# Stationary values in the sparse attention, identity products in TensorE's waits, earlier loads, and eight modulation tiles moved

## What is computed

```python
# first block: three branches over the same queries, and one over other queries
o_cmp, p_cmp = compressed_branch(qn, kc_cmp, vc_cmp)      # 31 compressed keys
o_sel = selected_branch(qn, ks_r, vs, sel_idx)
o_win = window_branch(qn, kw_r, vw)
o_nsa = g0 * o_cmp + g1 * o_sel + g2 * o_win
o_dsa = dsa_branch(qd, kd, v_d, qi_r, ki_r, wi)           # the 128 highest of the scored keys
x = x + concat(o_nsa * silu(z_n), o_dsa * silu(z_d)) @ w_out
# second block, layer i of 2; m = the 9 modulation vectors of layer i (mc: of the context)
m = split(silu(c) @ w_ada[i] + b_ada[i], 9)
h = h + 0.5 * m[2] * swiglu(modulate(rms_norm(h), m[0], m[1]), w13, w2)
z = modulate(rms_norm(h), m[3], m[4]) @ w_in[i]
h = h + m[5] * (concat(fourier, latent attention, spatial gating, pooling) @ w_out[i])
h = h + 0.5 * m[8] * swiglu(modulate(rms_norm(h), m[6], m[7]), w13, w2)
```

## Time and profile before

| | |
|---|---|
| median of 3 runs | 3424.47 us |
| the profiled execution | 3433.63 us, of which the profile's span is 3431.9 us |
| TensorE busy | 3162.7 us of the span (92%) |
| VectorE busy | 1799.3 us (52%) |
| ScalarE busy | 839.1 us (24%) |
| GpSimd busy | 127.0 us (4%) |
| mean granted TensorE clock | 0.928 of full |
| HBM | 82 GB/s over the span |

### The profile page before, as it was taken

One profiled execution on the slowest core, in us unless ns is written; L12 is line 12 of the kernel. 1 busy time (PEld: TensorE's weight loads), 2 busy tenths in 40 slices (PEclk: granted clock), 3 DMA queues, 4 the chain that ended last, 5 costly groups with the idle time before them and its releaser, 6 DMA issues. The chain is left out here.

```text
span 3431.9 us, 41816 instructions
## 1 busy us (share of the span) xinstructions
PE 3162.7 (92%) x17560; PEld 2715.4 (79%) x17560; DVE 1799.3 (52%) x2690; ACT 839.1 (24%) x1019; POOL 127.0 (4%) x96
## 2 busy tenths in 40 slices
PE   7847988999999978989999999999999888899998
PEld 6745877788888866667888888788888675589996
DVE  4656565475554654555444433764645555553434
ACT  3322223421111222313211212321211223132222
POOL 2320122000000000000000000000000000000000
PEclk9975557999999999989999999999999998899999
DMA  4342001343332312022323222343433210233231
GB/s 138 88 119 95 13 13 56 104 129 123 108 119 86 110 39 70 1 67 80 104 92 92 92 68 61 96 135 97 126 98 95 83 50 17 73 92 96 88 90 58
DMA packets 340316, 288.27 MB, mean 84 GB/s; under 512 B 12896, under 2 KB 315488, under 8 KB 339168
## 3 DMA queue, kind: packets, MB, share of 16 engines
q1 hardware_dynamic: 340192, 286.58, 28.2%
HBM read 279.72 MB, written 2.10 MB: 82 GB/s over the span
## 5 line engine op out<-in xcount | busy, mean ns | idle before, releaser
L2091 PE MATMUL PS<-x_hi_f,w_lo 128*128 128x258 f32 (+2 forms) x2560 | 622.3, 324 | 0.0
L2091 PE MATMUL PS<-x_lo_f,w_hi 128*128 128x258 f32 (+2 forms) x2560 | 622.0, 324 | 0.0
L2091 PE MATMUL PS<-x_hi_f,w_hi 128*128 128x258 f32 (+2 forms) x2560 | 620.8, 323 | 0.8 <-DVE w_lo L2137 0.8
L2091 PEld LDWEIGHTS PS<-x_hi_f,w_hi 128*128 128x128 f32 x2560 | 395.4, 189 | 43.9 <-issue 1.5
L2091 PEld LDWEIGHTS PS<-x_hi_f,w_lo 128*128 128x128 f32 x2560 | 395.3, 189 | 42.0
L2091 PEld LDWEIGHTS PS<-x_lo_f,w_hi 128*128 128x128 f32 x2560 | 393.2, 189 | 40.5
L2104 ACT ACTIVATE w_hi<-w_raw 128x2048 fp32r<-128x2048 f32 x131 | 250.0, 1908 | 498.4 <-PE PS L2091 496.7
L2091 PE MATMUL PS<-hid_hi_f,w_hi 128*128 128x512 f32 x1232 | 341.7, 347 | 0.9 <-DVE hid_lo_f L2157 0.9
L2091 PE MATMUL PS<-hid_hi_f,w_lo 128*128 128x512 f32 x1232 | 341.3, 347 | 0.0
L2091 PE MATMUL PS<-hid_lo_f,w_hi 128*128 128x512 f32 x1232 | 338.9, 345 | 0.0
L2137 DVE TENSOR_TENSOR w_lo<-w_raw,w_hi 128x2048 fp32r<-128x2048 f32 x131 | 299.6, 2287 | 35.1 <-ACT w_hi L2104 35.1
(11 more groups left out here) (323 smaller groups left out, 4409.9 us busy)
## 6 DMA issues: line engine op xcount, KB each, us to landing
w_raw<-in_w_ffn_dram SPq DMA_DIRECT2D x240, 512.0 KB, 5.1
sq_f<-in_w_ada_dram SPq DMA_DIRECT2D x120, 512.0 KB, 3.5
w_raw<-in_w_in_dram SPq DMA_DIRECT2D x46, 512.0 KB, 5.1
ada_room<-in_w_ada_dram SPq DMA_DIRECT2D x24, 512.0 KB, 3.5
w_raw<-in_w_out_dram SPq DMA_DIRECT2D x24, 512.0 KB, 5.1
w_raw<-in_w_ffn_dram SPq DMA_DIRECT2D x32, 384.0 KB, 3.9
ada_s<-in_conditions_dram SPq DMA_DIRECT2D x4, 1024.0 KB, 5.3
hT<-hT SPq DMA_DIRECT2D x56, 64.0 KB, 2.0
```

Source lines behind the costliest of these rows:

```text
L2091: last = nc.tensor.matmul(c.PS[:, 4 * q + 2 * w + m, 0:e - a], wt, xt[:, a:e], start=first, stop=end)
```

## The change

It touches seven places.

- **Values stationary.** In `weigh` the values of a group (128 x 66) are stationary and the exponentials of its four heads (128 x 512) moving: one product in place of four and the identity product. The result has 66 partitions and is accumulated in PSUM bank 4+g; ScalarE copies it to `OT` (`keep`, at its place among the exponentials), TensorE transposes it back per head (`back`, 8 transpositions per unit, issued after the second item of the next unit), and `finish` reads banks 6 and 7.
- **Row maxima in two parts.** VectorE does the first `k // items` maxima ahead of `finish`, the rest behind it.
- **Modulation.** `attend_first` loads and computes none of the tiles; tiles 16 to 71 (56) are in the first feed-forward block, with new shares. Vectors 0 and 1 are finished at the end of `attend_first`, vector 2 after step 3 of the feed-forward block.
- **Identity products** (`keep_warm(n, bank)`: n plain products of the identity with itself, 128 columns, into a bank that nobody reads) at the starts and ends of blocks.
- **Latent loads** (5 DMAs) are issued in `project_rows` instead of in `attention_mixer`; in the first layer into the half of `mixf` that is free there, in the second into a buffer of their own.
- **Head table** of the Fourier mixer: loaded at the same place.
- **Order** of the other loads there: sequence tables ahead of the pooling tables.

```diff
+    def keep_warm(self, n, bank):
+        for _ in range(n):
+            self.nc.tensor.matmul(self.PS[:, bank, 0:P], self.ident[:], self.ident[:], start=True, stop=True)
...
 (Normed.tensor)
+        self.c.keep_warm(8, 7)
         for j in range(KT // 2):
...
             last.then_inc(self.summed.sem, 1)
+            self.c.keep_warm(2 if j < KT // 2 - 1 else 36, 7)
...
 (project_rows, SP)
             if beside:
-                beside.loads.issue(sp)
+                for loads in beside.loads, *beside.ahead:
+                    loads.issue(sp)
...
 (attend_first)
+    OT = sb("o_turned", [66, GROUPS, 512])
-            for i in range(n_units):
-                share.load(sp, i)
...
-            def keep_warm(bank, first=False):
-                nc.tensor.matmul(c.PS[:, bank, 3 * P:4 * P], c.ident[:], c.ident[:], start=first, stop=True, skip_group_check=True)
-
             def weigh(n):
                 i, g, kt = items[n]
                 u = units[i]
                 pe.wait_ge(expd, n + 1)
-                if g == 0 and kt == 0 and i >= 2:
-                    pe.wait_ge(finished, i - 1)
-                for h in range(PER_GROUP):
-                    if h == 2:
-                        keep_warm(o_bank(i, g))
...
-                    last = nc.tensor.matmul(c.PS[:, o_bank(i, g), h * 66:(h + 1) * 66], e, v, start=(kt == 0 and h == 0),
-                                            stop=(kt == u.tiles - 1 and h == PER_GROUP - 1), skip_group_check=True)
+                if kt == 0 and i >= 1:
+                    pe.wait_ge(kept, GROUPS * (i - 1) + g + 1)
...
+                nc.tensor.matmul(c.PS[0:66, 4 + g, :], v, e, start=(kt == 0), stop=(kt == u.tiles - 1)).then_inc(weighed, 1)
+
+            def back(i):
+                pe.wait_ge(kept, GROUPS * (i + 1))
+                if i >= 1:
+                    pe.wait_ge(finished, i)
+                for g in range(GROUPS):
+                    for h in range(PER_GROUP):
+                        last = nc.tensor.transpose(c.PS[:, 6 + g, h * 66:(h + 1) * 66], OT[:, g, h * P:(h + 1) * P], c.ident[0:66, 0:66])
+                last.then_inc(backed, 1)
...
+                if m == 1 and i >= 1:
+                    back(i - 1)
...
 (ScalarE)
+            def keep(i, g):
+                act.wait_ge(weighed, last_item(i, g) + 1)
+                if i >= 1:
+                    act.wait_ge(backed, i)
+                nc.scalar.activation(OT[:, g, :], c.PS[0:66, 4 + g, :], ACT.Copy).then_inc(kept, 1)
...
                 exp(n)
+                if n == first[i] and i >= 1:
+                    keep(i - 1, 1)
+                if n == last_item(i, 0) + 1:
+                    keep(i, 0)
...
 (VectorE)
+                k = units[i + 3].row_items if i + 3 < n_units else 0
+                early = k // (first[i + 1] - first[i])
+                if early:
+                    maxes(i + 3, range(early))
                 if i >= 1:
                     finish(i - 1)
-                if i + 3 < n_units:
-                    maxes(i + 3)
+                if k > early:
+                    maxes(i + 3, range(early, k))
...
-                share.vector(dve, ch, i)
...
 (ffn, TensorE)
+            c.keep_warm(8, 4 * ((s0 + 1) % 2))
             up_products(0)
...
+            pe.wait_ge(ring.drained, s0 + n_steps + 1)
+            c.keep_warm(14, 4 * ((s0 + n_steps) % 2))
...
 (attention_mixer, SP; the five loads now in RankNorms' ahead)
-                    loads.issue(sp)
...
 (attention_mixer, TensorE, behind the last item)
+                    c.keep_warm(20, 6)
...
 (Fourier.tensor)
+        self.c.keep_warm(4, 7)
         self.head_in.wait(pe)
...
 (fourier_and_pooling, SP)
-            for loads in (ft.head_in, pl.loads, ft.seq_in, later):
+            for loads in (ft.seq_in, pl.loads, later):
...
 (Gating.finish, TensorE)
+                    c.keep_warm(4, 7)
                     self.loads.wait(pe)
...
                         last.then_inc(self.mixed.sem, 1)
+                    c.keep_warm(6, 7)
...
 (finish_output, TensorE)
+                c.keep_warm(6, 7)
                 for j in range(KT // 2):
...
+                    c.keep_warm(2, 7)
+                c.keep_warm(18, 7)
...
-ADA_PLAN = {(0, 0): (ada_shares(2, 1), [(0, m) for m in range(3, 9)]),
+ADA_PLAN = {(0, 0): ([2] * 8 + [1] * 4 + [2] * 8 + [1, 1, 1, 2] + [2] * 6 + [1, 1, 1, 0], [(0, m) for m in range(3, 9)], (3, [(0, 2)])),
```

More of the change, by code:

```diff
@@ L1090, in wait_bank, with last_item @@
             pe.wait_ge(moved, ip + 1)
-    def o_bank(i, g):
-        return 4 + 2 * (i % 2) + g
+    def last_item(i, g):
+        return first[i] + (g + 1) * units[i].tiles - 1
     with nc.Block() as block:
@@ L1178, in _ @@
                     row(i, j)
-                    keep_warm(4 + j % 4, True)
+                    nc.tensor.matmul(c.PS[:, 4 + j % 4, 0:P], c.ident[:], c.ident[:], start=True, stop=True)
                 if i >= 1:
@@ L1193, in _ @@
             weigh(len(items) - 1)
+            back(n_units - 1)
         @block.scalar
@@ L1238, in _ @@
                     move(i + 2)
+            keep(n_units - 1, 1)
         @block.gpsimd
@@ L1290, in _, with maxes @@
             ch = c.dve.on(dve)
-            def maxes(i):
+            def maxes(i, some=None):
                 u = units[i]
@@ L1295, in maxes @@
                     dve.wait_ge(turned, i - 2)
-                for j in range(u.row_items):
+                for j in some or range(u.row_items):
                     dve.wait_ge(rowed, row_first[i] + j + 1)
@@ L1772, in vector, with finish @@
             dot.then_inc(ada.done, 1)
-    def finish(self, dve, ch):
+    def finish(self, dve, ch, some=None):
         ada, nc = self.ada, self.ada.nc
-        if not self.finish_list:
+        which = some or self.finish_list
+        if not which:
             return
         dve.wait_ge(ada.small_in, 32)
-        dve.wait_ge(ada.done, self.tiles[-1].stop)
-        mods = [(l, v, m) for l, m in self.finish_list for v in range(2)]
+        dve.wait_ge(ada.done, max(l * N_MOD * KT + (m + 1) * KT for l, m in which))
+        mods = [(l, v, m) for l, m in which for v in range(2)]
         at = lambda l, v, m: ada.c.mod[:, l, v, m * KT:(m + 1) * KT]
@@ L1818, in first_block @@
             with scope(nc) as sb:
-                later = AdaShare(c.ada, s_c, share.bufs, share.product, [0, 1, 1, 0, 1, 1, 0, 0, 0, 0, 0, 0, 1, 1, 1, 1], [(0, m) for m in range(3)], share)
-                attend_first(c, sb, rows, O, Q, KK, KL, KKc, KLc, Vx, Vc, scores, sc_at, tri, dram, later)
+                attend_first(c, sb, rows, O, Q, KK, KL, KKc, KLc, Vx, Vc, scores, sc_at, tri, dram, share)
 class Refill:
@@ L1972, in invert, with ffn @@
         ch.link(self.c.nc.vector.reciprocal(self.inv[:], self.inv[:]))
-def ffn(c, sb, ring, x, w13, w2, gates, spans, tag, after=None, shares=None, finish=()):
+def ffn(c, sb, ring, x, w13, w2, gates, spans, tag, after=None, shares=None, finish=(), soon=None):
     nc = c.nc
@@ L2168, in body @@
                         share.vector(dve, c.dve.on(dve), s - s0)
+                        if soon and s - s0 == soon[0]:
+                            share.finish(dve, c.dve.on(dve), soon[1])
             x.vector(dve, c.dve.on(dve), ring.rest_second(dve, s0))
@@ L2269, in mix_layer, with __init__ @@
         project_cols(c, ring, x, dram["w_out_2"][l], ALL_TILES, spans, drain, after)
+class Latent:
+    SIZE = 4 * MH * QKW + 2 * MH * 64 + 2 * SEQ
+    def __init__(self, c, l, room, dram):
+        n = 2 * MH * QKW
+        at = [0, n, 2 * n, 2 * n + 2 * MH * 64, 2 * n + 2 * MH * 64 + SEQ]
+        self.w_uq, self.w_uqs = (room[0:96, a:a + n].rearrange("p (j n) -> p j n", j=2) for a in at[0:2])
+        self.w_ukv = room[0:KV_RANK, at[2]:at[3]].rearrange("p (h t n) -> p h t n", h=MH, t=2)
+        self.cos, self.sin = (room[0:QKW, a:a + SEQ] for a in at[3:5])
+        self.loads = Loads(c, "mla_in", [(self.w_uq, dram["w_uq"][l].rearrange("(j p) n -> p j n", p=96)),
+                                         (self.w_uqs, dram["w_uq_swapped"][l].rearrange("(j p) n -> p j n", p=96)),
+                                         (self.w_ukv, dram["w_ukv"][l].rearrange("p (h t n) -> p h t n", h=MH, t=2)),
+                                         (self.cos, dram["rope_cos"]), (self.sin, dram["rope_sin"])])
 class RankNorms:
-    def __init__(self, c, sb, x, cqT, ckvT, spans, g_q, g_kv):
+    def __init__(self, c, sb, x, cqT, ckvT, spans, g_q, g_kv, ahead):
         self.c = c
+        self.ahead = ahead
         gains = sb("g_q", [96, 2]), sb("g_kv", [KV_RANK, 1])
```

44 lines of the change are left out of this document (20 added, 24 removed).

## The result

The changed kernel takes **3344.84 us** in the median of four runs (3338.50 to 3346.53); the kernel before took 3430.4 beside it (3423.39 to 3438.24). The ratio is 0.9747, 95% interval 0.9717 to 0.9776. The profiled execution took 3344.92 us, its span is 3343.1 us, the mean clock 0.961. Against the profiled execution of before that is 88.7 us less, where 66 were forecast. A second set of runs of the same kernel gave 3346.46 (3339.78 to 3346.78). In the sets of the experiments the kernel before took 3432 to 3442 in the median; so experiments from different sets are compared here only where they lie well apart, and the intervals of the ratios say how well each stands against the kernel before.

A forecast was written before the change was run, and what follows sets the result against it. The first attention was taken as bound by TensorE, busy at a mean clock of 0.62. From a 3424.5 us median, -32 us in the attention and -34 at the seams gave 3358 us, range 3315 to 3402.

The forecast's parts named there:

- The stretches: First attention cut into seven time windows, each given a new length: sum -49.5 us, -32 after charges for clock drops.
- At an equal clock the change is a loss: First attention: `weigh` saves 18 or 12 us, `back` adds 48 or 26; loss of 30 (low) or 14 us (high).
- VectorE then sets the pace: First attention: a unit costs selection rounds plus 1.8 us plus remaining items, where that exceeds TensorE's own sum.
- `keep` ... hidden: First attention: ScalarE's 32 added copies, some 20 us on top of 76 busy of 266, cost no time.
- Modulation tiles hidden in the feed-forward block: First feed-forward block: eight moved tiles, 22 us of VectorE, are covered by TensorE and cost 0; uncovered, 22 us.
- Transpositions and the clock: First attention: `back`'s transpositions do not cost the clock, going by a profile row at 1.00 against the skill's rule.
- The seams: Starts and ends of blocks: identity products and earlier loads gain 3.8 + 6 + 17.6 + 2.6 + 3.8 = 34 us.
- Fourier: Fourier mixer: head wait shrinks but the sequence tables' wait takes over; between 0 and -3.8, taken as -1.9 us per layer.
- Rival 1: First attention: VectorE binds less and the clock holds; attention -60 us, in all 3331; chance 0.15.
- Rival 2: First attention: no gain, as the clock falls at each stall and each `back`; 3391 us; chance 0.15.
- rival 3: Slower: the clock stays at 1.2 GHz through all of the first attention; 3443 us; chance 0.04.
- rival 4: Seams give only -5 us: identity products overrun at the low clock or loads weren't the last wait; 3387; chance 0.08.

The follow-up runs named there:

- the first experiment: The changed kernel with the first attention in its old form, modulation tiles still in the feed-forward block, loads and identity products as changed: 3371.58 us, ratio 0.979.
- the best one: The changed kernel with selection rounds laid between the row maxima on VectorE, and ScalarE moving the maxima before its copies: 3312.87 us, ratio 0.9631.

## Why the prediction was right, and where its sizes were off

**"Faster, by the clock": right.** The range held the time and the forecast case, not a rival, is what happened; it lies 13 us below the number. That is partly luck: the number starts from 3424.5 for the kernel before, which took 3430.4 beside the changed one, so 66 us were forecast and 85.6 came. Of 88.7 us between the profiled executions 44 are the attention (32 forecast), some 42 the seams (34 forecast), and 2.6 lie ahead of both, in code that the change leaves alone.

**The stretches.** Forecast 14, 18, 21.5, 16, 32, 54 and 37 us; measured 16.8, 20.1, 22.5, 18.1, 30.7, 54.9 and 34.8. Sum 192.8 (before rounding) against 197.9, with the clock's penalties already in the measured ones. I charged 18 us for them on top; 5 were due. That over-charge is the 12 us.

**"At an equal clock the change is a loss": wrong.** The step that failed is `back` = 1.6 us high and 3.0 low, taken from plain products with 66 moving columns. Measured 0.66 and 1.09, and 12.9 us for all 16 units where 26 or 48 stood. The saving was put too low as well: an item fell from 1.81 to 1.57 us at the high clock, 0.24 and not 0.17, some 16 us for 68. Against it stand 16 x 0.66 = 10.6, so at an equal clock the change is a gain of some 6 us, and at the low clock, with the 18 of the forecast's 0.26 an item against 16 x 1.09 = 17.4, it is even. It pays mostly by the clock, but not only. The run with plain products had about the forecast's price, 1.90. Whether the new form would still have won at it is open: by the profiles yes (225.8 against 240.7), by the medians it is 2 us (3369.39 against 3371.58), inside the scatter.

**The clock: right, and shown from both sides.** The new product is as forecast (1.57 an item against 1.55). Added 128-column products raised the clock in the old form as well, from 0.62 to 0.80, and took the gain themselves. The new form has the same clock with useful work.

**VectorE then sets the pace: right.** The wait of 3.59 us behind eight rounds is the step as written. What I did not see is that the order, not the amount, was the price: 20 us were to be had by interleaving, as many as by leaving 21 rounds out.

**"`keep` ... hidden": wrong.** The forecast had GpSimd wait for the moved maxima "a unit ahead of need", and put ScalarE's new order at nothing. TensorE's waits for ScalarE's move rose from 1.3 to 10.3 us, and with the move put first 12 us of the time came back. The gain of the attention was larger than forecast in spite of this.

**Modulation tiles hidden in the feed-forward block: right.** 560.8 us with them, 561.0 without. In the attention they cost 10 us of the stretch in the new form, of 22 us of work, and at least 6 in the old one.

**Transpositions and the clock: right.** The forecast held with the row at clock 1.00 against the Trainium skill, "TensorE: Matmul & The Clock Gate", Part 4. The plain products in place of the transpositions left the clock at 0.78 against 0.80, and it rose to 1.0 at 546.10 behind transpositions alone. The measurement decides against the rule for these float32 transpositions.

**The seams.** By the undo of the identity products the norms gave 1.6 + 1.8 (forecast 3.8), the feed-forward openings 5.3 (6), the second attention's start 4.9 (2.6), of which 2.6 were lost again in Fourier. Latent loads: forecast 17.6, measured 7.3 + 6.9 + 1.6 = 15.8. **The mis-sized term is Fourier**, -1.9 in each layer: I let the sequence loads' wait take the place of the head's. The undo of the loads shows 5.7 and 6.2, of which 2.0 come back in the projection of layer 0, so 9.9 net where 3.8 stood: 6 of the 8 us that the seams gave beyond the forecast. Both waits shrank, the head's to nothing and that for `w_fnet` from 6.9 to 3.7 us over the two layers, since the sequence loads now stand first in their queue. In layer 0 the clock also stayed up through both; in layer 1 it was low until 2850.1, in the first head products. Gating and output, put at 0, gave 4.1 us in layer 0 and lost 2.2 in the projection behind it, with the clock low from 1451 to 1458 behind a wait of 3.3; the undo of the identity products shows the same 4.1 and 2.3, so they are worth about 2 there and nothing in layer 1.

**The rivals.** Rival 1 (VectorE binds less) is out: the run without 7 of the 16 rounds took 21 us less, and the attention came to -44, not -60. Rival 2 (nothing in the attention) is out by the first experiment, rival 3 by the first long unit at 0.80, rival 4 by the two undos at the seams, 15 and 23 us.

## What to carry to other kernels

Where TensorE is busy at the low clock, look at how many columns stream behind each load: give the wide operand the moving side, and a form that saves a few us at an equal clock can be worth over a tenth of the stage (27 to 38 of 241 us here). When it speeds up, look next at blocks of work on the other in-order engines: a long block ahead of a result that TensorE awaits can hold it back each time (3.6 us of waiting behind eight rounds here), and laying it between the short results cost nothing and gave 20 us; so did ordering ScalarE by who is waited for (12 us). Identity products pay only inside a wait and at their full price: count the passes of the data type, and size them to end before the wait does (shorter ones at the last projection were not tried).

## What the runs showed of the hardware that was not expected

- A float32 transposition is one instruction where a plain float32 product of the same shape is two: 0.66 against 1.90 us for eight.
- Transpositions bring the granted clock up and keep it there as products do (0.5 to 1.0 behind transpositions alone at 546.10; 0.80 with them, 0.78 with products in their place).
- Short waits are dear: removing 8.1 us of waits of 1.4 to 1.8 us took 13.7 us off the stretch, since the clock rose from 0.84 to 0.90.
- The same code at the same place differs from run to run by some us through where the clock falls: 202.4, 202.3, 202.5 and once 198.8 us for the new attention; 171.8 and 176.2 for the best one.
